# Norm sums, residual order, head of the input projection and softmax division of a two-layer hybrid trunk

## The chip, the cores and the metric

The kernel runs on one core of one Trainium2 chip. The metric is the device time of one execution in microseconds (us), lower is better.

## The reference

All arithmetic is float32. x is (1, 512, 1024); there are two layers, and mem is (1, 256, 1024).

```python
for l in range(DEPTH):
    h = rms_norm(x, norm_mix_pre[l])
    (c_q, c_kv, k_rope, ml_q, ml_k, ml_v, ml_o, ml_i, ml_f,
     sw_q, sw_k, sw_v) = jnp.split(h @ w_in[l], splits, axis=-1)
    # A: 8 heads of latent attention, dense causal; B: 4 mLSTM heads, chunkwise;
    # C: 4 heads of dilated window attention; outputs concatenated
    ... # x += rms_norm(concat @ w_out, norm_mix_post)
    ... # x += rms_norm(cross_attention(rms_norm(x, norm_x_pre), rms_norm(mem)), norm_x_post)
    ... # x += rms_norm(swiglu(rms_norm(x, norm_ffn_pre)), norm_ffn_post)

def rms_norm(x, g):
    return x * lax.rsqrt(jnp.mean(x * x, axis=-1, keepdims=True) + EPS) * g
```

The attention of groups A and C ends in `softmax(s) @ v`; the softmax divides by the sum of the exponentials of a query's row.

## The kernel before, in words

**Layout.** Activations are feature-major: x is 8 tiles (index k) of 128 features by 512 tokens. A weight unit is 128 by 1024 floats, the weights of one output tile of 128 features (index m) with its 8 k steps; there are 128 units per layer (N_UNITS). They pass through a ring of RING = 4 slots: SP loads `raw`, ACT copies it rounded to `w_hi`, DVE makes `w_lo = raw - w_hi` (line 1180, `lo_until(n)`), and TensorE does three matmuls per k step, hi by hi, lo by hi, hi by lo (lines 499 to 501, `three`, `project_step`). A slot is free when TensorE has used its unit (`unit_used`); SP loads unit u when the split of unit u - 4 is done. Activations are split alike: ACT makes `h_hi` (`scaled_hi`, line 861), DVE makes `h_lo` (`scaled_lo`, line 1167). A float32 matmul that isn't split shows as two matmul records.

**Norms.** The sum over features of a norm is taken on TensorE. ACT squares the 8 tiles into two buffers of `sq` in turn (`square`, line 869), DVE adds each to `acc` (`add_square`, lines 1159 and 1161), and `norm_sum` (line 546) multiplies ones by `acc` into bank 7; every partition then has the sum. ACT takes Ln and Exp(-0.5 .) of it (`make_rstd`, lines 885 and 887). There are six such norms per layer: mix_pre, mix_post, x_pre, x_post, ffn_pre and ffn_post. For mix_pre and ffn_pre the rstd is applied behind the matmuls, so that these can start before the norm is known. q and kv have sums of their own (`latent_sum`, line 554).

**Gaps.** A sublayer ends in `post` on ACT (square, and copy with gain, of each output tile), then `norm_sum`, `make_rstd`, and `residual` on DVE: y[k] *= rstd (line 1240), x[k] += y[k] (line 1244), with `between(k)` in each turn, here the h_lo of the next sublayer (`ffn_input`, `next_input`) one tile late, and its squares' adds. The next sublayer's first matmuls run k by k over a few units at once: HEAD = 3 units of the input projection, 4 units of the FFN (`gate_up_step`). Their order is written out in the program of each engine, with semaphores between engines. In layer 0 the first units and the x tiles arrive in turn from DMA, and ACT and DVE take two tiles of x behind each unit.

**Behind the head.** The input projection has 10 tiles (IN_FM) in 6 banks. DVE takes each tile (`take`, line 1231) times mix_rstd and does the gates, convolutions and so on between takes; take m first makes the splits up to unit m + 3.

**Paired heads** (groups A and C, 6 pairs per layer, 4 blocks of 128 queries per pair). In step s TensorE makes the scores of two units (`pair_scores`, line 721), DVE masks them and takes the maximum (`pair_mask`, line 1489), ACT takes the exponential with its sum into `stat[:, 1]` (`pair_exp`, line 1066), DVE takes the reciprocal and scales the probabilities (`pair_divide`, lines 1499 and 1500), TensorE transposes them two steps later (`pair_transposes`, line 734), ACT copies them (`pair_copy`, line 1056). After four blocks `pair_out` (line 745) multiplies by v for both heads, each in its own 64 rows of a bank; ACT and DVE split the result into h_hi and h_lo (`pair_hi`, line 1045; `pair_lo`, line 1477). The out projection waits for the last of them.

## Time and profile before

| | |
|---|---|
| median of 3 runs | 1746.42 us (1743.43 to 1747.57) |
| profiled execution | 1746.7 us, span 1744.9 us |
| TensorE busy (matmul) | 1631.1 us, 93% |
| VectorE busy | 981.3 us, 56% |
| ScalarE busy | 737.3 us, 42% |
| mean granted clock of TensorE | 0.971 |
| chain that ended last | TensorE 85%, VectorE 9%, issue 3%, ScalarE 2% |

The span is the time from the first to the last instruction. The chain is followed back from the last instruction, at each step to what released it. The granted clock is 1.00 at 2.4 GHz and 0.50 at 1.2 GHz. PE is TensorE, DVE is VectorE, ACT is ScalarE, SP issues the DMAs. L12 is line 12 of the kernel.

### The profile page before, as it was taken

Reading aid. Unit: us, or ns where it says so; the run is one execution under the profiler, and the core shown is the slowest. Engines: PE = TensorE matmul, PEld = TensorE weight load, DVE = VectorE, ACT = ScalarE, POOL = GpSimd, SP = SyncE. Lnnn points to the kernel's source line nnn. Section 1 sums busy time; section 2 is a strip of 40 time slices with the busy share of each in tenths; the row PEclk is TensorE's granted clock in tenths of the full one; section 3 lists DMA queues with packets and bytes.
Section 4 is the critical chain, followed back from the end, with each engine's and each line's share of the span. In section 5 each row is a group of like instructions: output and inputs, shape, how many; then the busy total and the mean of one; then the engine's idle time right before and its main releaser. Section 6 shows DMA issues by size and latency. Waiting matters only on the chain.

```text
span 1744.9 us, 18819 instructions
## 1 busy us (share of the span) xinstructions
PE 1631.1 (93%) x7044; PEld 1244.2 (71%) x7044; DVE 981.3 (56%) x1612; ACT 737.3 (42%) x1244; POOL 5.7 (0%) x6
## 2 busy tenths in 40 slices
PE   6999889999989999999989998799999899999996
PEld 5765547877768888888767554487768688888884
DVE  5767874674365555532287678657553755555223
ACT  5522664544444444432244227545353444444221
POOL 0000000000000000000000000000000000000000
PEclk9998999999999999999999989999999999999998
DMA  5311003351213333333213110034403123333321
GB/s 223 109 60 37 13 1 109 109 162 55 61 49 97 97 97 107 99 109 97 85 49 109 49 37 1 17 128 146 121 25 88 51 91 101 105 97 101 105 73 48
DMA packets 38826, 144.62 MB, mean 83 GB/s; under 512 B 4304, under 2 KB 4432, under 8 KB 38224
## 3 DMA queue, kind: packets, MB, share of 16 engines
q1 hardware_dynamic: 38736, 143.43, 26.8%
q8 instruction: 56, 0.92, 0.2%
q14 instruction: 34, 0.28, 0.1%
HBM read 141.31 MB, written 2.10 MB: 82 GB/s over the span
## 4 chain that ended last, share of the span: by engine, by line
PE 85%; DVE 9%; issue 3%; ACT 2%; DMA 0%; SPq 0%; DVEq 0%; ACTq 0%
PE bank L499 24%; PE bank L501 24%; PE bank L500 24%; PE bank L721 2%; PE bank L745 2%; PE bank L794 2%; PE bank L784 1%; PE bank L647 1%; PE bank L655 1%; DVE x L1244 1%; PE bank L734 1%; DVE p_mix L1500 1%; DVE tn_x L1209 1%; DVE w_lo L1180 1%; PE bank L546 1%
## 5 line engine op out<-in xcount | busy, mean ns | idle before, releaser
L499 PE MATMUL bank<-h_hi,w_hi 128*128 128x512 f32 x1312 | 529.1, 403 | 41.2 <-DVE h_lo L1167 22.0
L1180 DVE TENSOR_TENSOR w_lo<-raw,w_hi 128x1024 fp32r<-128x1024 f32 x256 | 312.9, 1225 | 441.5 <-ACT w_hi L850 429.2
L500 PE MATMUL bank<-h_lo,w_hi 128*128 128x512 f32 x1312 | 517.6, 395 | 0.0
L501 PE MATMUL bank<-h_hi,w_lo 128*128 128x512 f32 x1312 | 517.3, 394 | 0.0
L850 ACT ACTIVATE w_hi<-raw 128x1024 fp32r<-128x1024 f32 x256 | 268.3, 1050 | 203.5 <-PE bank L501 193.7
L499 PEld LDWEIGHTS bank<-h_hi,w_hi 128*128 128x128 f32 x1312 | 249.7, 190 | 110.3 <-issue 34.4
L500 PEld LDWEIGHTS bank<-h_lo,w_hi 128*128 128x128 f32 x1312 | 250.1, 191 | 54.7 <-issue 3.4
L501 PEld LDWEIGHTS bank<-h_hi,w_lo 128*128 128x128 f32 x1312 | 250.4, 191 | 53.3
L501 PE MATMUL bank<-a_hi,w_lo 128*128 128x512 f32 x352 | 139.1, 395 | 0.0
L499 PE MATMUL bank<-a_hi,w_hi 128*128 128x512 f32 x352 | 139.0, 395 | 0.0
L500 PE MATMUL bank<-a_lo,w_hi 128*128 128x512 f32 x352 | 139.0, 395 | 0.0
L1161 DVE TENSOR_TENSOR acc<-acc,sq 128x512 f32<-128x512 f32 x84 | 58.1, 691 | 103.9 <-ACT sq L869 102.9
L869 ACT ACTIVATE sq<-bank 128x512 f32<-128x512 f32 x48 | 28.7, 598 | 153.9 <-PE bank L501 153.9
L1136 ACT ACTIVATE a_hi<-sq 128x512 fp32r<-128x512 f32 x44 | 27.8, 632 | 140.8 <-DVE sq L1576 140.8
L500 PEld LDWEIGHTS bank<-a_lo,w_hi 128*128 128x128 f32 x352 | 66.1, 188 | 16.1
L501 PEld LDWEIGHTS bank<-a_hi,w_lo 128*128 128x128 f32 x352 | 66.1, 188 | 16.0
L499 PEld LDWEIGHTS bank<-a_hi,w_hi 128*128 128x128 f32 x352 | 66.1, 188 | 16.0
L1131 ACT ACTIVATE acc<-sq 128x512 f32<-128x512 f32 x44 | 27.8, 632 | 110.1 <-DVE sq L1569 110.1
L988 ACT ACTIVATE w_ml<-w_ml 128x512 f32<-128x512 f32 (+3 forms) x32 | 15.0, 470 | 113.3 <-DVE w_ml L1410 113.3
L721 PE MATMUL bank<-k_mla,q_mla 128*128 128x128 f32 (+3 forms) x128 | 43.1, 461 | 5.3 <-DVE stat L1489 5.3
L1056 ACT ACTIVATE pt_mix<-bank 128x128 f32<-128x128 f32 (+3 forms) x96 | 39.4, 438 | 19.9 <-PE bank L734 18.3
L499 PE MATMUL bank<-m_hi,w_hi 128*128 128x256 f32 x128 | 37.9, 296 | 5.7 <-DVE w_lo L1180 5.0
(186 smaller groups left out, 1922.7 us busy)
## 6 DMA issues: line engine op xcount, KB each, us to landing
raw<-w_in SPq DMA_DIRECT2D x256, 512.0 KB, 3.6
x<-x_in SPq DMA_DIRECT2D x4, 512.0 KB, 8.3
mem<-mem_in SPq DMA_DIRECT2D x2, 1024.0 KB, 4.9
out<-x SPq DMA_DIRECT2D x4, 512.0 KB, 2.6
consts<-c_in SPq DMA_DIRECT2D x1, 1728.0 KB, 13.1
mem_sq<-mem_in SPq DMA_DIRECT2D x1, 1024.0 KB, 5.7
gains<-g_in SPq DMA_DIRECT2D x1, 80.0 KB, 3.3
```

The source lines that it names most:

```text
L499: pe.matmul(out_ap, l_hi, r_hi, start=start, stop=False)
L500: pe.matmul(out_ap, l_hi, r_lo, start=False, stop=False)
L501: return pe.matmul(out_ap, l_lo, r_hi, start=False, stop=stop)
L721: pe.matmul(score_ring[u % 4][:, 0:n], hd["q"][:, qb * P:n], hd["k"][:, 0:n], start=True, stop=True).then_inc(mix_at["scored"], 1)
L745: mm = pe.matmul(outs[pair % 2][64 * i:64 * i + 64, kb * P:SEQ], mix_head(2 * pair + i)["v"](kb), pt_mix[:, i, kb, kb * P:SEQ], start=(kb ...
L794: mm = pe.matmul(outs[c][:, :], v_x[:, kb, col:col + P], pt_x[:, head % 2, kb, :], start=(kb == 0), stop=(kb == 1))
L850: act.activation(w_hi[:, s, :], raw[:, s, :], ACT.Copy).then_inc(split_hi, 1)
L869: act.activation(sq[:, c % 2, 0:width], src, ACT.Square).then_inc(squared, 1)
L1056: act.activation(pt_mix[:, i, 0:m, qb * P:(qb + 1) * P], turned[i][:, 0:m * P].rearrange("p (b q) -> p b q", q=P), ACT.Copy).then_inc(mix_ ...
L1131: done(act.activation(sig, gate_up, ACT.Exp, scale=-1.0), act_step)
L1161: ins = dve.tensor_tensor(acc[:, :], acc[:, :], sq[:, c % 2, :], ALU.add)
L1180: dve.tensor_tensor(w_lo[:, s, :], raw[:, s, :], w_hi[:, s, :].bitcast(F32), ALU.subtract)\
```

## The change

- **Norm sums.** DVE adds only the first 7 squares. TensorE multiplies ones by `acc` and then, into the same sum, by the eighth square. The squares' waits are counted anew.
- **Residual.** x[0] is updated ahead of y[1]'s scaling; `ffn_input(k)` and `next_input(k)` make h_lo of tile k in turn k (before: of k - 1), the last split of the ring moves behind the first h_lo, and `make_rstd` goes ahead of that unit's w_hi on ACT.
- **Dummy matmuls.** Behind the sums of x_post and (in layer 0) ffn_post TensorE does four float32 matmuls of 128 by 512 whose result nobody reads (`keep_busy`).
- **Head.** HEAD = 4 units; TensorE waits for the first FFN units one by one. In layer 0 the k steps of the head follow the list FIRST_HEAD, and ACT's squares and DVE's adds come behind all tiles.
- **Paired heads.** `pair_divide` is gone. DVE takes the reciprocals of a pair's 8 units at once (`pair_invert`); behind `pair_out` TensorE spreads them over a bank with 8 matmuls of a broadcast column by the identity; ACT copies that to `rstd` (`pair_spread`), DVE multiplies the pair's output by it into `sq` (`pair_scale`), and h_hi and h_lo are made from `sq`.
- Three small tiles change their place in SBUF.

```diff
-HEAD = 3
+HEAD = 4
...
+FIRST_HEAD = ([(k, m) for k in range(2) for m in range(1)] + [(k, 1) for k in range(2)]
+              + [(k, m) for k in (2, 3) for m in range(2)] + [(k, 2) for k in range(4)]
+              + [(k, m) for k in (4, 5) for m in range(3)] + [(k, 3) for k in range(6)]
+              + [(k, m) for k in (6, 7) for m in range(HEAD)])
...
-                        pe.matmul(norm_bank[:, 0:width], const(C_ONES), acc[:, 0:width], start=True, stop=True)\
-                          .then_inc(norm_summed, 1)
+                        pe.matmul(norm_bank[:, :], const(C_ONES), acc[:, :], start=True, stop=False)
+                        pe.wait_ge(squared, count(squared, layer, squares_before(name) + KT))
+                        pe.matmul(norm_bank[:, :], const(C_ONES), sq[:, (layer * N_SQUARES + squares_before(name) + KT - 1) % 2, :],
+                                  start=False, stop=True).then_inc(norm_summed, 1)
...
+                    def keep_busy(n):
+
+                        for _ in range(n):
+                            pe.matmul(outs[0][:, :], const(C_ONES), const(C_ROPE_Q, SEQ), start=True, stop=True)
...
-                            pe.wait_ge(mix_at["probs"], count(mix_at["probs"], layer, u + 1))
+                            pe.wait_ge(mix_at["exped"], count(mix_at["exped"], layer, u + 1))
...
                         mm.then_inc(mix_at["out"], 1)
+                        pe.wait_ge(mix_inverted, count(mix_inverted, layer, pair + 1))
+                        for qb in range(TB):
+                            for i in range(2):
+                                u = 2 * (TB * pair + qb) + i
+                                mm = pe.matmul(outs[(pair + 1) % 2][64 * i:64 * i + 64, qb * P:(qb + 1) * P],
+                                               stat[:, 2, u:u + 1].broadcast_to([P, 64]), const(C_IDENT),
+                                               start=True, stop=True)
+                        mm.then_inc(mix_spread, 1)
...
+                    def pair_spread(pair):
+
+                        act.wait_ge(mix_spread, count(mix_spread, layer, pair + 1))
+                        act.activation(rstd[:, :], outs[(pair + 1) % 2][:, :], ACT.Copy).then_inc(mix_spread_copied, 1)
...
-                    split_until(U_FF + 4)
                     make_rstd("x_post", D_MODEL)
+                    split_until(U_FF + 4)
...
+                        scale(0)
+                        for k in range(KT):
+                            dve.wait_ge(y_scaled, count(y_scaled, layer, first + k + 1))
+                            done(dve.tensor_tensor(x[:, k, :], x[:, k, :], y[:, k, :], ALU.add), x_updated)
+                            if k + 1 < KT:
+                                scale(k + 1)
+                            if between is not None:
+                                between(k)
...
                     done(dve.memset(conv_in[:, :, 0:3], 0.0), pads_set)
+                    lo_until(HEAD + 1)
                     dve.wait_ge(rstd_ready, count(rstd_ready, layer, 1))
...
+                    def pair_scale(pair):
+
+                        dve.wait_ge(mix_at["out"], count(mix_at["out"], layer, pair + 1))
+                        dve.wait_ge(mix_spread_copied, count(mix_spread_copied, layer, pair + 1))
...
+                        done(dve.tensor_tensor(sq[:, pair % 2, :], outs[pair % 2][:, :], rstd[:, :], ALU.mult), mix_scaled)
...
-                    lo_until(U_FF + RING)
+                    lo_until(U_FF + RING - 1)
 
                     def ffn_input(k):
 
+                        scaled_lo(layer, "ffn_pre", k, G_FFN_PRE)
+                        lo_until(U_FF + RING)
                         if k >= 1:
-                            scaled_lo(layer, "ffn_pre", k - 1, G_FFN_PRE)
                             add_square(layer, "ffn_pre", k - 1)
```

## Rows read from the trace of the kernel before

**Rows 1.** Who waited for whom, TensorE: waiter, releaser, us in total, times, longest.

```profile
PE bank L734 <- DVE p_mix L1500: 13.6, 14, 1.7
PE bank L734 <- DVE tn_mix L1500: 6.2, 8, 1.2
```

**Rows 2.** Timeline of the gap before layer 0's FFN: start, us, engine, line, operation, idle before.

```profile
494.03 0.60 ACT L869 ACTIVATE sq<-bank 128x512 f32<-128x512 f32 x1 [3.31 <-PE bank L501]
...
495.41 1.12 PE L546 MATMUL bank<-acc,consts 128*128 128x512 f32 x2 [1.42 <-DVE acc L1161]
...
497.95 1.29 DVE L1240 TENSOR_TENSOR y_x<-y_x,rstd 128x512 f32<-128x512 f32 x2 [0.47 <-ACT rstd L887]
...
499.17 0.69 DVE L1244 TENSOR_TENSOR x<-x,y_x 128x512 f32<-128x512 f32 x1
...
501.22 0.75 DVE L1167 SCALAR_TENSOR_TENSOR h_lo<-x,gains,h_hi 128x512 fp32r<-128x512 f32 x1
...
502.12 0.77 PE L499 MATMUL bank<-h_hi,w_hi 128*128 128x512 f32 x1 [5.58 <-DVE h_lo L1167]
...
503.79 0.75 DVE L1167 SCALAR_TENSOR_TENSOR h_lo<-x,gains,h_hi 128x512 fp32r<-128x512 f32 x1
...
505.30 0.69 DVE L1240 TENSOR_TENSOR y_x<-y_x,rstd 128x512 f32<-128x512 f32 x1
...
505.91 0.69 DVE L1244 TENSOR_TENSOR x<-x,y_x 128x512 f32<-128x512 f32 x1
...
506.63 0.75 DVE L1167 SCALAR_TENSOR_TENSOR h_lo<-x,gains,h_hi 128x512 fp32r<-128x512 f32 x1
```

**Rows 3.** TensorE in one microsecond: stretch, its length, busy, matmuls, granted clock.

```profile
504.00:505.00 1.00, 1.00 (x4) 0.50 0.00 0
```

**Rows 4.** The chain that ended last, in order of time: start, us, what.

```profile
33.75 0.86 PE bank L546 x2
...
71.95 1.72 PE bank L554 x4
...
523.64 0.86 PE bank L546 x2
...
869.12 1.14 PE bank L546 x2
...
897.51 0.86 PE bank L546 x2
...
932.24 1.72 PE bank L554 x4
...
1354.16 1.14 PE bank L546 x2
...
1383.04 0.86 PE bank L546 x2
```

**Rows 5.** Timeline at the start of the kernel, ACT and DVE.

```profile
7.54 0.72 ACT L861 ACTIVATE h_hi<-x,gains 128x512 fp32r<-128x512 f32 x1 [1.98 <-DMA x<-x_in]
...
8.38 0.75 DVE L1167 SCALAR_TENSOR_TENSOR h_lo<-x,gains,h_hi 128x512 fp32r<-128x512 f32 x1 [1.45 <-ACT h_hi L861]
```

**Rows 6.** Timeline behind the head of layer 1, DVE.

```profile
899.85 0.69 DVE L1231 TENSOR_TENSOR q_mla<-bank,mix_rstd 128x512 f32<-128x512 f32 x1 [4.43 <-ACT mix_rstd L887]
...
906.41 1.23 DVE L1180 TENSOR_TENSOR w_lo<-raw,w_hi 128x1024 fp32r<-128x1024 f32 x1
```

**Rows 7.** Timeline at the x_pre norm of layer 0, DVE.

```profile
359.12 1.54 DVE L1209 SCALAR_TENSOR_TENSOR tn_x<-x,gains,rstd 128x512 f32<-128x512 f32 x2 [2.13 <-ACT rstd L887]
```

**Rows 8.** Timeline and groups by form, paired heads, layer 0.

```profile
221.76 2.37 PE L745 MATMUL bank<-pt_mix,v_mla 128*64 128x512 f32 x16
...
272.35 0.50 PE L499 MATMUL bank<-h_hi,w_hi 128*128 128x512 f32 x1 [1.50 <-DVE h_lo L1477]
...
L745 PEld LDWEIGHTS bank<-pt_mix,v_mla 128*64 128x64 f32 x128 | 8.5, 136 | 12.9 <-issue 7.4 <-ACT pt_mix L1056 4.4
```

**Rows 9.** TensorE's share and clock, last 16 us of the stage (same columns, all engines).

```profile
254.80:271.00 16.20, 13.04 (x61) 6.29 (x60) 7.40 (x24) 7.91 (x23) 0.00 (x0) 0.75 0.01 2
```

More of the change, by code:

```diff
@@ L226, with added_before @@
 N_SQUARES = sum(k for n, k in NORMS if n not in LATENT)
+SUMMED = [n for n, _ in NORMS if n not in LATENT]
+N_ADDED = (KT - 1) * len(SUMMED)
+def added_before(name):
+    return (KT - 1) * SUMMED.index(name)
 N_NORMED = sum(k for _, k in NORMED)
@@ L568, in _ @@
                         pe.wait_ge(emptied_act, count(emptied_act, layer, 0))
-                    for k in range(KT):
-                        after_norm("mix_pre")(k)
-                        for m in range(HEAD):
-                            project_step("in", m, k, tiles(h_hi), tiles(h_lo))
+                    for k, m in [(k, m) for k in range(KT) for m in range(HEAD)] if layer else FIRST_HEAD:
+                        if m == 0:
+                            after_norm("mix_pre")(k)
+                        project_step("in", m, k, tiles(h_hi), tiles(h_lo))
                     pe.wait_ge(consts_loaded, 16)
@@ L836, in _ @@
                     norm_sum("ffn_post")
+                    if layer + 1 < DEPTH:
+                        keep_busy(4)
             @block.scalar
@@ L1189, in _ @@
                     scaled_lo(0, "mix_pre", k, G_MIX_PRE)
+                for k in range(KT):
                     add_square(0, "mix_pre", k)
@@ L1237, in residual, with scale @@
                         first = scaled_before(name)
-                        for k in range(KT + 1):
-                            if k < KT:
-                                dve.tensor_tensor(y[:, k, :], y[:, k, :], rstd[:, :], ALU.mult)\
-                                   .then_inc(y_scaled, 1)
-                            if k >= 1:
-                                dve.wait_ge(y_scaled, count(y_scaled, layer, first + k))
-                                done(dve.tensor_tensor(x[:, k - 1, :], x[:, k - 1, :], y[:, k - 1, :], ALU.add),
-                                     x_updated)
-                                if between is not None:
-                                    between(k - 1)
+                        def scale(k):
+                            dve.tensor_tensor(y[:, k, :], y[:, k, :], rstd[:, :], ALU.mult).then_inc(y_scaled, 1)
+                        scale(0)
+                        for k in range(KT):
+                            dve.wait_ge(y_scaled, count(y_scaled, layer, first + k + 1))
[4 more added lines that the diff above has]
+                                between(k)
                     def tiles(t):
@@ L1476, in pair_lo @@
                         dve.wait_ge(mix_at["out_hi"], count(mix_at["out_hi"], layer, pair + 1))
-                        done(dve.tensor_tensor(h_lo[:, tile, :], outs[pair % 2][:, :], h_hi[:, tile, :].bitcast(F32),
+                        done(dve.tensor_tensor(h_lo[:, tile, :], sq[:, pair % 2, :], h_hi[:, tile, :].bitcast(F32),
                                                ALU.subtract), mix_at["out_lo"])
```

85 lines of the change are left out of this document (50 added, 35 removed).

## The prediction

> **What bounds the kernel now.** I read the waits of TensorE first. The two lines of the softmax division are the largest item that the change touches outside the gaps: 13.6 + 6.2 = 19.8 us over both layers, in which transposes wait for a scaled tile [rows 1]. Then the timeline of one gap, from the last x_post square to the first matmul of the FFN. The reader is to see a chain in which every link starts when the one before lands: square 494.03, sum 495.41, scaling 497.95, residual 499.17, h_lo 501.22, matmul 502.12 [rows 2]. From there a new h_lo comes every 506.63 - 503.79 = 2.84 us [rows 2], and the clock that TensorE was granted is the lower of its two levels, 1.2 GHz, with four matmuls in a microsecond; before the fall it had done nothing but the 1.12 us of the norm sum since 494.0 [rows 2, 3]. Last the chain of waits, which gives the milestones: the norm sum behind the head at 33.75 and 897.51, the latent sum behind tile 8 of the input projection at 71.95 and 932.24, the ffn_pre sum at 523.64 and 1383.04 [rows 4]. Outside gaps, heads and attention TensorE sets the pace.
>
> The sum is made against the profiled execution, 1746.7 us (span 1744.9, 1.8 around it); the median of the runs is 1746.42, so I take 0.3 off at the end. A measurement of this kernel tells 0.2%, 3.5 us, from no change.
>
> **Price of a tile.** 932.24 - 897.51 = 34.73 us hold one norm matmul (0.86), eight one-column matmuls (about 1.0, estimated) and six tiles [rows 4], so a tile costs 5.45 and three matmuls, one k step, 0.68.
>
> **Norm sums.** Each of 12 gets a second matmul of 0.86 [rows 4]. In a gap the matmul over acc runs under the square, and the one over the square starts when the square lands, about 0.69 after 494.03, and not 495.41 - 494.03 = 1.38 after it [rows 2]: 0.69 won. Elsewhere TensorE or what waits for the sum pays 0.86.
>
> **The gap before the FFN.** Scale, scale, add took 499.17 - 497.95 = 1.22; scale and dependent add take about 0.72 (the step from an add to its reader, 505.91 to 506.63): 0.50 won. From the add to h_lo it was 501.22 - 499.17 = 2.05. Now ACT starts h_hi 0.72 after the add, and h_lo comes 8.38 - 7.54 = 0.84 later [rows 5]: 1.56, 0.49 won. The first matmul comes at 502.12 - 0.69 - 0.50 - 0.49 = 500.44. The four dummy matmuls (3.4 us) fill 495.6 to 499.0, so I expect 2.4 GHz there. They end 1.4 us ahead of the h_lo that TensorE needs, and cost nothing; if the sum came 1.4 later they would stand in the way. The Trainium skill (page "TensorE: Matmul & The Clock Gate", section "What's actually happening") says that the throttled state is the default and activity releases it; by that rule alone the gap would also give back its slow matmuls, 1.6 us here. The trace agrees on the fall.
> But VectorE becomes the limit. A tile's period was 2.84, of which the scale took 505.91 - 505.30 = 0.61 [rows 2]; now the scale hides inside the 0.84 wait for h_hi: 2.84 - 0.61 + 0.84 = 3.07, against 4 x 0.68 = 2.72 of TensorE. The last w_lo split, until now hidden before the rstd, goes behind the first h_lo (1.23 by itself [rows 6]; I take 1.14 to the next start, an estimate, since neighbours overlap by some 0.1 where the reader is another engine). SP asks for a unit's weights when the split of four units before is made, so these loads start about 3 us later; they are used some 20 us on, and their cover is large. First h_lo 499.54, split from 500.32, second add 501.46, second h_lo 503.02, eighth 503.02 + 6 x 3.07 = 521.44. Its first three matmuls end 0.90 + 0.68 later, 523.02, where it was 523.64: 0.62 won. In layer 1 the gap sits 1354.16 - 495.41 = 858.75 later [rows 2, 4], so 1381.77 against 1383.04: 1.27 won. Less 2 x 0.86 for ffn_pre: **+0.2**.
>
> **The gap before layer 1.** It begins 869.12 - 495.41 = 373.71 after the other [rows 2, 4]. Eighth h_lo 895.15, its matmuls from 896.05, four units each, sum at N = 898.77, where three units got there at 897.51. Behind it: 1.72 for two matmuls, tile 4, the one-column matmuls, then tile 5, whose split VectorE makes only after its third take. That was 906.41 - 899.85 = 6.56 after the first take, and the take 899.85 - 897.51 = 2.34 after the sum [rows 4, 6]; now N + 3.20 + 6.56 - 1.14 (tile 4's split is made ahead) = N + 8.62, usable 1.33 later (a split and 0.1), where TensorE comes at N + 8.15. A stall of **1.8** that no head of three had. Latent sum at N + 1.72 + 5 x 5.45 + 1.0 + 1.8 = N + 31.8 = 930.5, against 932.24: **+1.7**.
>
> **The first head.** TensorE starts at 8.38 + 0.85 = 9.23 as before [rows 5], 0.85 being the 0.75 of h_lo and 0.1. With the squares moved behind all splits, ACT and VectorE make h_lo and w_lo faster than TensorE uses them in the new order. 32 steps take 21.8; the first 4.4 us at half clock add 2.2 (an estimate by the 3 us from 502.12 past 504 that it stayed low with dense work [rows 2, 3]; bounds 1.7 and 3.9), waiting for the second split 0 to 0.5. N = 33.5, latent sum at N + 31.8 + 3.5 (the memory's eight matmuls: 71.95 - 33.75 less 34.73) = 68.8, against 71.95: **+3.2** (1.5 to 3.9).
>
> **Sums in the dense part, and the waits added.** mix_post and x_pre stand in series: the second rstd is followed at once by VectorE, which had waited 2.13 for it at 359.12 [rows 7], and its h_lo chain ends last. 2 x 2 x 0.86 = **-3.4**; a gain in its place is excluded, the last add dropped was ahead of time. The new waits of ACT's squares on the previous sum stand behind an rstd that needed the same sum, so nothing queues there. The end of the kernel wins 0.69 and loses 7 x 0.12 (0.72 for 0.61, a dependent pair): **-0.15**.
>
> **The paired heads.** The division moves behind the product. VectorE loses 48 reciprocals and 48 scalings per layer, and of the 9.9 us of waits per layer [rows 1] I give back 6.8, an estimate: two waits of up to 0.7 in each pair, a pair more of them in the first and the last; the rest returns as waits for ACT, which must wait for the spread and copy it before the next pair's copies and exponentials, queued behind. VectorE's new wait for the last exponential of a pair has only the mask of scores behind it that TensorE has not made yet: nothing. Against it 8 matmuls of 64 by 128 per pair, which no row shows. Lower bound: the product's eight have 2560 columns in 2.37 us [rows 8], at its rate 1024 columns take 0.92. Upper bound: 16 loads one after the other, 16 x 0.136 = 2.2 [rows 8]. Their columns are short as the loads are, so I take 1.3, six times 7.8. At the end of the stage the out projection waited 1.50 [rows 8]; a copy of 512 columns on ACT (0.6 to 0.7, like ACT's other passes) and a scaling on DVE (0.72) more make 2.9: 1.4 lost. 6.8 - 7.8 - 1.4 = -2.4 per layer. The stage already ran at 0.75 of the clock in its last 16 us [rows 9]; a longer wait at its end may cost more, denser work before it may save: -0.3 each (bounds -3 and +3). Both layers: **-5.4**.
> The Trainium skill (same page, section "Part 3: Packing small matmuls — row/col tiling") says that matmuls in different column groups run at once, but that a weight load overlaps a matmul only when its row group differs. The first half agrees with the product, 2.37 us for columns that one by one would take five norm matmuls' time, 4.3. The second, which speaks against this change since all rows are used, would make the price the upper bound or more; in the product loads do hide.
>
> **Sum.** 0.2 + 1.7 + 3.2 - 3.4 - 0.15 - 5.4 = -3.9: 1746.7 + 3.9 - 0.3 = **1750.3 us**.
>
> **Rivals.** (1) Faster than before: the spread is cheap. At 0.92 each 12 x 0.38 = 4.6 us come back, and if the denser stage keeps its clock, 16.2 x 0.25 = 4.0 less what the tail still loses, say 3 per layer: 1750.3 - 4.6 - 6 = 1739.7. It decides on this side once the spread and the clock together give back 7.4. For: the product's rate. Against: short matmuls, the end's longer wait. 0.24.
> (2) Loads in series, 2.2 each: 12 x 0.9 more, 1761. For: nothing in the product shows 128 columns alone. Against: loads there hide. 0.12.
> (3) The reorder does not slow VectorE (period 2.84): 6 x 0.23 = 1.4 us more in each of three gaps, 1746. For: the parts sum to it. Against: the 0.84 must pass between two instructions of one tile. 0.10.
> **How the numbers follow.** My forecast has 0.54. Its own range is 1746 to 1755 (the bounds of the first head, the stall ahead of tile 5, and the clock in the pairs), half of it within 0.2% of 1746.4. Over all I give 1740 to 1758, which leaves out (2) and the far part of (1). Faster: (1), 0.24. Within 0.2%: 0.27 of the forecast and (3), 0.37. Slower: 0.27 and (2), 0.39.
>
> **What would show it.** First FFN matmul 6.4 us after the last square's start (was 8.1), at full clock, h_lo period 3.07; N near 33.5 and 898.8; a wait of 1.8 for w_lo ahead of tile 5; x_pre rstd 1.7 later against the end of the out projection; the spread's duration; transposes that no longer wait for VectorE. Wrong if the spread is under 1 us or over 2, or if the stall ahead of tile 5 is absent.

## The result and the profile after

The changed kernel takes 1736.17 us (median of 6 runs, 1733.40 to 1738.99) against 1746.58 of the kernel before (6 runs); the ratio is 0.9945, 95% interval 0.9932 to 0.9957. Measured again beside later kernels it was 1737.34 us, 0.9947 (0.9929 to 0.9966). It is faster by 0.5%, some 9.5 us; the forecast was 1750.3, and the measured time lies below the whole range. The profiled run took 1733.7 us (span 1731.9), 13.0 less than the profiled run before, so part of what two profiles differ by is chance. A second profile of the changed kernel took 1740.4 us: its two stages of paired heads took 76.27 us each, where they take 73.37 in the profile shown here.

The chain that ended last, changed kernel (start, us, what), against [rows 4]:

```profile
33.48 0.86 PE bank L563 x2
42.05 1.24 DVE w_lo L1233
...
70.48 1.72 PE bank L573 x4
...
518.91 0.89 PE bank L563 x2
...
891.56 0.87 PE bank L565 x2
899.26 1.24 DVE w_lo L1233
924.20 1.72 PE bank L573 x4
```

The sum behind the first head came at 33.48 (forecast 33.5), the latent sum at 70.48, only 1.5 earlier than before. The chain now passes through a split on VectorE in both layers, at 42.05 and 899.26: the stall ahead of tile 5 that the forecast had at 1.8 us.

The gap before the FFN of layer 0 (timeline: start, us, engine, line, operation, idle before), against [rows 2]:

```profile
490.54 0.60 ACT L909 ACTIVATE sq<-bank 128x512 f32<-128x512 f32 x1 [3.33 <-PE bank L518]
491.20 1.12 PE L565 MATMUL bank<-sq,consts 128*128 128x512 f32 x2
492.15 3.60 PE L580 MATMUL bank<-consts 128*128 128x512 f32 x8
...
493.73 0.69 DVE L1294 TENSOR_TENSOR y_x<-y_x,rstd 128x512 f32<-128x512 f32 x1 [5.19 <-ACT rstd L927]
494.46 0.69 DVE L1299 TENSOR_TENSOR x<-x,y_x 128x512 f32<-128x512 f32 x1
...
495.19 0.72 ACT L897 ACTIVATE h_hi<-x,gains 128x512 fp32r<-128x512 f32 x1 [0.54 <-DVE x L1299]
...
495.95 0.75 DVE L1220 SCALAR_TENSOR_TENSOR h_lo<-x,gains,h_hi 128x512 fp32r<-128x512 f32 x1
496.73 1.22 DVE L1233 TENSOR_TENSOR w_lo<-raw,w_hi 128x1024 fp32r<-128x1024 f32 x1
496.80 0.47 PE L516 MATMUL bank<-h_hi,w_hi 128*128 128x512 f32 x1 [1.05 <-issue]
...
499.36 0.75 DVE L1220 SCALAR_TENSOR_TENSOR h_lo<-x,gains,h_hi 128x512 fp32r<-128x512 f32 x1
...
502.09 0.75 DVE L1220 SCALAR_TENSOR_TENSOR h_lo<-x,gains,h_hi 128x512 fp32r<-128x512 f32 x1
```

From the last square to the FFN's first matmul it is 496.80 - 490.54 = 6.26 us, where it was 8.09 (forecast 6.4). The sum starts 0.66 behind the square, the add follows its scaling by 0.73, and the dummies of L580 run from 492.15 to 495.75. VectorE's h_lo comes 2.73 behind the one before (499.36 to 502.09) and 3.00 later on (forecast 3.07). The split of the last unit, at 496.73, stands behind the first h_lo, as forecast. In the microsecond that had the lower clock [rows 3], the clock is up (stretch, its length, busy, matmuls, granted clock, DMA):

```profile
504.00:505.00 1.00, 1.00 (x6) 1.00 0.00 0
```

The paired heads. First the waits of TensorE (us in total, times, longest), against [rows 1]; then the end of the stage in layer 0, against [rows 8]; then the clock of the stage's end and of the 3.5 us behind it, against [rows 9] (stretch, its length, busy time of PE, PEld, which is the weight loads, DVE, ACT and POOL, then clock, DMA):

```profile
PE bank L758 <- ACT pt_mix L1105: 10.6, 18, 1.2
```

```profile
260.00 2.37 PE L769 MATMUL bank<-pt_mix,sw_v 128*64 128x512 f32 x16 [0.74 <-ACT pt_mix L1105]
262.21 1.04 PE L777 MATMUL bank<-consts,stat 128*64 128x128 f32 x16
263.30 0.60 ACT L1095 ACTIVATE rstd<-bank 128x512 f32<-128x512 f32 x1 [3.35 <-PE bank L777]
264.09 0.69 DVE L1542 TENSOR_TENSOR sq<-bank,rstd 128x512 f32<-128x512 f32 x1 [6.12 <-ACT rstd L1095]
...
266.30 0.79 PE L516 MATMUL bank<-h_hi,w_hi 128*128 128x512 f32 x1 [3.05 <-DVE h_lo L1548]
```

```profile
254.80:266.30 11.50, 5.42 (x50) 3.46 (x48) 3.49 (x8) 6.80 (x16) 0.00 (x0) 1.00 0.00 0
266.30:269.80 3.50, 3.50 (x8) 2.79 (x9) 0.00 (x0) 0.10 (x1) 0.00 (x0) 0.51 0.70 222
```

The two lines of [rows 1] are gone, 19.8 us; in their place stand 10.6 us for ACT's copies. The spread (L777, 16 records for 8 matmuls) takes 0.97 us to the next instruction inside the stage (220.47 to 221.44 in layer 0), and 1.04 as a row. The chain at the end is the forecast's: spread, copy, scale, h_hi, h_lo, a wait of 3.05 where it was 1.50. The last product runs at full clock, 2.37 us; the out projection behind the wait starts at half clock, its matmuls 0.43 us apart.

These rows alone do not say why the kernel became faster and not slower. The largest difference between the traces lies in a stretch that the forecast did not touch. From the ffn_pre sum to the ffn_post sum it was 345.64 and 345.71 us in the two layers (523.48 to 869.12 in layer 0, the records of the sum over acc) and is 341.32 and 341.31 now, about 0.8 of which is only the new norm sums (the sum over acc starts earlier, and ffn_pre has a matmul more). The groups by form (count | busy us, mean ns of one), before and after:

```profile
L500 PE MATMUL bank<-h_lo,w_hi 128*128 128x512 f32 x1312 | 517.6, 395 | 0.0
L499 PE MATMUL bank<-a_hi,w_hi 128*128 128x512 f32 x352 | 139.0, 395 | 0.0
```

```profile
L517 PE MATMUL bank<-h_lo,w_hi 128*128 128x512 f32 x1312 | 517.1, 394 | 0.0
L516 PE MATMUL bank<-a_hi,w_hi 128*128 128x512 f32 x352 | 136.9, 389 | 0.0
```

The matmuls over h_lo are as they were; those over a_hi (the down projection) went from 395 to 389 ns. Their starts say the same, before and after:

```profile
760.21 0.40 PE L501 MATMUL bank<-a_hi,w_lo 128*128 128x512 f32 x1
760.44 0.39 PE L499 MATMUL bank<-a_hi,w_hi 128*128 128x512 f32 x1
760.67 0.40 PE L500 MATMUL bank<-a_lo,w_hi 128*128 128x512 f32 x1
```

```profile
760.10 0.39 PE L516 MATMUL bank<-a_hi,w_hi 128*128 128x512 f32 x1
760.33 0.39 PE L517 MATMUL bank<-a_lo,w_hi 128*128 128x512 f32 x1
760.55 0.39 PE L518 MATMUL bank<-a_hi,w_lo 128*128 128x512 f32 x1
```

Averaged over the records of a stretch, the distance from start to start in the down projection was 233.3 ns and is 226.7 ns, at full clock in both; in gate and up it is 226.7 in both. 1056 matmuls by 6.6 ns are 7.0 us.

### The profile page after: what moved, and what is told of

It reads as the page before. It is cut to its first block, busy times and chain, and to the rows that moved or that the text cites. A ratio compares the mean times of both kernels' runs of the same rounds, so it can differ in the third digit from the quotient of the medians.

```text
span 1731.9 us, 19052 instructions
## 1 busy us (share of the span) xinstructions
PE 1643.7 (95%) x7284; PEld 1258.7 (73%) x7284; DVE 933.6 (54%) x1432; ACT 739.2 (43%) x1256; POOL 5.7 (0%) x6
## 4 chain that ended last, share of the span: by engine, by line
PE 81%; DVE 9%; ACT 7%; issue 2%; DMA 0%; SPq 0%; DVEq 0%; ACTq 0%
PE bank L516 23%; PE bank L518 23%; PE bank L517 23%; PE bank L826 2%; PE bank L769 2%; DVE x L1299 2%; PE bank L816 1%; ACT pt_mix L1105 1%; ACT p_mix L1115 1%; PE bank L671 1%; DVE h_lo L1220 1%; PE bank L679 1%; ACT h_hi L897 1%; PE bank L745 1%; DVE w_lo L1233 1%
## 5 line engine op out<-in xcount | busy, mean ns | idle before, releaser
L1214 DVE TENSOR_TENSOR acc<-acc,sq 128x512 f32<-128x512 f32 x72 | 49.7, 691 | 75.9 <-ACT sq L909 75.0
L897 ACT ACTIVATE h_hi<-x,gains 128x512 fp32r<-128x512 f32 x32 | 22.8, 723 | 41.6 <-DVE x L1299 38.8
```

Source lines behind the costliest of these rows:

```text
L897: act.activation(h_hi[:, k, :], x[:, k, :], ACT.Copy, scale=gains[:, layer, g + k:g + k + 1])\
L1214: ins = dve.tensor_tensor(acc[:, :], acc[:, :], sq[:, c % 2, :], ALU.add)
```

## The experiments

All ratios are against the kernel before, run beside. "From start to start" is the mean over the records of one stretch of a trace.

**The move alone.** The three small tiles that change their place in SBUF, and nothing else:

```
         gains = sb("gains", [P, DEPTH, N_GAINS])
+        mem_rstd = sb("mem_rstd", [P, N_MEM])
+        stat = sb("stat", [P, 3, MIX_UNITS])
+        acol = sb("acol", [P, TB, ML_HEADS])
         raw = sb("raw", [P, RING, UNIT])
...
         rstd = sb("rstd", [P, SEQ])
-        mem_rstd = sb("mem_rstd", [P, N_MEM])
-        stat = sb("stat", [P, 3, MIX_UNITS])
-        acol = sb("acol", [P, TB, ML_HEADS])
```

> The kernel before with nothing but three small tiles (mem_rstd, stat, acol: 1024 + 576 + 64 = 1664 B of each partition) allocated ahead of raw instead of behind rstd. Theory A (placement): in the profile of the changed kernel the down-projection's matmuls start every 0.2268 us, in that of before every 0.2335; the move puts w_hi 73,728 B ahead of a_hi instead of 75,392, a whole multiple of 256 instead of 128 more. 1056 such matmuls x 0.0067 = 7.1 us: I expect 1739.5 us and a mean of 389 ns for the matmuls over a_hi and a_lo. Theory B (the pitch comes from something else in the change, the clock or what ACT and VectorE do meanwhile): no change, 1746.6 us, mean 395 ns.

Measured: 1738.41 us, ratio 0.9954 (0.9941 to 0.9967), 7 to 8 us faster. The group of its profile:

```profile
L499 PE MATMUL bank<-a_hi,w_hi 128*128 128x512 f32 x352 | 136.9, 389 | 0.0
```

The stretch from ffn_pre to ffn_post is 342.14 and 342.22 us, 3.5 less in each layer. Theory A holds: the larger part of the whole gain is this move.

**The changed kernel without the move** (the same lines undone):

> The changed kernel with those three tiles back behind rstd, all else kept. Theory A (placement): the 7.1 us are given back, 1743.3 us, mean 395 ns over a_hi and a_lo; the changed kernel would then be worth only 3.3 us without its placement. Theory B: 1736.2 us and 389 ns.

Measured: 1742.53 us, 0.9978 (0.9969 to 0.9987), 395 ns over a_hi and a_lo. As theory A had it. So the rest of the change wins some 3 to 4 us, where my sum had it lose 3.9.

**The division alone.** The kernel before with the paired heads' part of the diff (the new functions pair_invert, pair_scale, pair_spread, the spread's matmuls, pair_divide gone):

```
-                            pe.wait_ge(mix_at["probs"], count(mix_at["probs"], layer, u + 1))
+                            pe.wait_ge(mix_at["exped"], count(mix_at["exped"], layer, u + 1))
...
+                        for qb in range(TB):
+                            for i in range(2):
...
+                                mm = pe.matmul(outs[(pair + 1) % 2][64 * i:64 * i + 64, qb * P:(qb + 1) * P],
+                                               stat[:, 2, u:u + 1].broadcast_to([P, 64]), const(C_IDENT),
+                                               start=True, stop=True)
```

> The kernel before with nothing but the paired heads' softmax division moved behind the product (invert once per pair, spread, scale). Theory A (from the two traces: the stage took 73.6 us before and 69.0 after in layer 0, less 0.9 for the half-speed start of the out projection behind it): 3.7 to 4.6 us faster per layer, 1737 to 1739.5 us, a spread of 0.90 us per pair. Theory B (my forecast on record, spread 1.3 and 5.4 lost in both layers): 1752 us.

Measured: 1746.12 us, 1.0001 (0.9989 to 1.0013). Neither theory: nothing won and nothing lost.

**Tiles between the weights and h_hi.** A direct test of what in the placement counts:

```
         w_lo = sb("w_lo", [P, RING, UNIT], F32R)
+        stat = sb("stat", [P, 3, MIX_UNITS])
+        acol = sb("acol", [P, TB, ML_HEADS])
...
         mem_rstd = sb("mem_rstd", [P, N_MEM])
-        stat = sb("stat", [P, 3, MIX_UNITS])
-        acol = sb("acol", [P, TB, ML_HEADS])
```

> The kernel before with stat and acol (640 B) allocated between w_lo and h_hi instead of behind rstd: w_hi and w_lo stay where they are, h_hi, h_lo, sq, acc and rstd move up by 640 B (128 more than a multiple of 256), mem_rstd and a_hi stay. Theory A1 (what counts is where the moving tile lies relative to the weights, modulo 256 B): the matmuls over h_hi and h_lo go from 0.2268 to 0.2335 us apart, 3936 x 0.0067 = 26 us slower, 1773 us, and those over a_hi stay at 0.2335. Theory A2 (the address of the weights alone, or of a_hi alone, counts): no change, 1746.6 us. Theory B: no change.

Measured: 1768.18 us, 1.0126 (1.0110 to 1.0142), 22 us slower. Its matmuls over h, which were 226.7 ns apart, and their group:

```profile
560.38 0.39 PE L501 MATMUL bank<-h_hi,w_lo 128*128 128x512 f32 x1
560.61 0.40 PE L499 MATMUL bank<-h_hi,w_hi 128*128 128x512 f32 x1
560.84 0.39 PE L500 MATMUL bank<-h_lo,w_hi 128*128 128x512 f32 x1
...
L500 PE MATMUL bank<-h_lo,w_hi 128*128 128x512 f32 x1312 | 524.7, 400 | 0.0
```

233.3 ns from start to start; those over a stayed at 233.3. Later in this trace both are 232.4 (over h from 1420 to 1460 us, over a in layer 1), with every tile where it was. Theory A1: the distance between the tile that streams and the tile that is loaded as weights. Absolute addresses are ruled out by the move alone, where w_hi and h_hi went up together by 1664 B and the matmuls over h kept 226.7.

**Move and division together** (the edits of the first and third experiment):

> The kernel before with the three tiles moved and the division moved, nothing else. With the move alone the kernel took 1738.4 us. The profile of the division alone shows the stage from the first scores to the first matmul of the out projection at 73.4 us in both layers, against 77.2 before (3.8 won in each), the out projection behind it 1.5 longer in each (it starts at half clock behind a wait of 3.0), and the stretch ahead of the stage 2.5 longer in each, with a lower granted clock. Theory C (those 2.5 are what the division does to the kernel, by the clock): nothing won again, 1738.4 us. Theory D (they were that arrangement's luck with the clock): 2 x (3.8 - 1.5) = 4.6 won, 1733.8 us.

Measured: 1736.91 us, 0.9946 (0.9930 to 0.9962). Between the theories: the median is 1.5 us better than with the move alone, which the intervals don't tell from nothing.

**The changed kernel with the old division** (the diff's paired part undone):

> The changed kernel with the division back where it was, all else kept, the move of the tiles too. Theory C (the division wins nothing): 1736.2 us. Theory D: 4.6 slower, 1740.8 us. My forecast on record (it costs 5.4): 1730.8 us.

Measured: 1738.95 us, 0.9955 (0.9936 to 0.9973), 1.6 to 2.8 us slower than with the new one. My recorded price is refuted, and the full 4.6 of theory D is not shown either.

**Without the dummies:**

```
                     norm_sum("x_post")
-                    keep_busy(4)
...
                     norm_sum("ffn_post")
-                    if layer + 1 < DEPTH:
-                        keep_busy(4)
```

> The changed kernel without its four dummy matmuls in the three gaps. Theory E (they hold the clock): the first matmuls of the FFN and of layer 1 run at half speed again as in the kernel before, where the windows of 10 us behind the gaps stood at 0.73, 0.53 and about 0.7 of the clock; 1.6 us by my forecast's figure for each of three gaps, 1741 us. Theory F (the h_lo period of VectorE covers it, or the clock stays up anyway): 1736.2 us.

Measured: 1731.73 us, 0.9920 (0.9903 to 0.9936): not slower, but 4 us faster. The clock fell as theory E says (TensorE by stretches of 2 us behind the gap; length, busy, matmuls, clock, DMA):

```profile
498.00:500.00 2.00, 2.00 (x6) 0.50 0.58 225
500.00:502.00 2.00, 2.00 (x10) 0.91 0.03 8
```

and the gap, from the sum over acc to the ffn_pre sum, grew by 0.2 us only, 28.41 to 28.62. The first k step over four units took 5.1 us at half clock (495.43 to 500.54) and ended 1.8 us behind the moment at which the second h_lo was made. From there TensorE took 2.7 us for a k step and VectorE 3.00 for an h_lo, so TensorE caught up, all but 0.2 us. Theory F for the gap. Where the other 3 to 4 us come from is taken up below.

**Single sums outside the gaps, and an earlier split:**

```
+IN_GAP = ("x_post", "ffn_post")
...
+                        if name not in IN_GAP:
+                            pe.matmul(norm_bank[:, :], const(C_ONES), acc[:, :], start=True, stop=True)\
+                              .then_inc(norm_summed, 1)
+                            return
...
-                            lo_until(m + RING)
+                            lo_until(HEAD + 2 if m == 1 else m + RING)
```

> The changed kernel with two things made otherwise: the norm sums of mix_pre, mix_post, x_pre and ffn_pre are one matmul over the sum of all eight squares again (x_post and ffn_post keep two), and VectorE splits unit 5 ahead of its second take behind the head. By the stages of the two traces each of the eight second matmuls costs TensorE 0.77 to 0.86 us, 6.5 in all; the stall ahead of tile 5 is 1.6 in layer 0, with half speed behind it for about 4 us (1.5 to 2 more), and 1.2 to 1.5 in layer 1: 4.5. I expect 1736.2 - 11 = 1725 us. Rival: the stall goes to tile 6, whose split waits for the convolution (loses the 4.5 again): 1730 us.

Measured: 1727.99 us, 0.9893 (0.9874 to 0.9912), 8 to 9 us faster than the changed kernel where 11 were expected. The stretch from the mix_post sum to the x_pre sum is 0.85 and 0.86 shorter in the two layers, the next one 0.89 and 0.86: the price of a second matmul. From the sum behind the head to the latent sum it went from 37.00 to 33.78 us and from 33.50 to 29.95, of which 0.86 is the sum; so the stall cost 2.4 and 2.7 us, not 1.8. Its idle part is 1.6 to 1.7; the rest is the half clock behind it, in the changed kernel (same columns):

```profile
42.00:43.00 1.00, 0.00 (x0) 1.00 0.00 0
44.00:46.00 2.00, 2.00 (x8) 0.61 0.71 236
46.00:48.00 2.00, 2.00 (x6) 0.54 0.07 27
```

**Dummies at the end of the pairs instead of in the gaps,** on the last kernel:

```
+                    keep_busy(3)
                     pe.wait_ge(mix_at["out_lo"], count(mix_at["out_lo"], layer, MIX_PAIRS))
...
-                    keep_busy(4)
...
-                    if layer + 1 < DEPTH:
-                        keep_busy(4)
```

> The last kernel (single norm sums outside the gaps, unit 5 split early; 1728.0 us) with the four dummy matmuls of the gaps left out and three put behind the last pair's spread, where TensorE waits 3.05 us for h_lo and then runs its first eight matmuls at half speed, 0.43 us apart instead of 0.23, from 266.3 to 269.6. Theory G (these dummies keep the clock, and TensorE is what sets the pace behind them): 1.6 won in each layer, and 0.2 lost in each gap, 1728.0 - 3.2 + 0.6 = 1725.4 us. Rival: as in the gaps, what is won is covered by another engine: 1728 us.

Measured: 1723.60 us, 0.9870 (0.9850 to 0.9889), the fastest median here, 23 us below the kernel before. These dummies write into another bank (`wide[0]`). The out projection starts at full clock (timeline, layer 0):

```profile
258.90 1.04 PE L789 MATMUL bank<-consts,stat 128*64 128x128 f32 x16
259.88 2.84 PE L592 MATMUL bank<-consts 128*128 128x512 f32 x6
263.00 0.50 PE L524 MATMUL bank<-h_hi,w_hi 128*128 128x512 f32 x1 [0.28 <-DVE h_lo L1558]
```

From the start of the last matmul of the products to the mix_post sum it is 51.38 us in layer 0 and 52.11 in layer 1, against 52.07 to 53.37 in the profiles of the same stage without these dummies. The gain is a little above what theory G expected, but two things changed at once, the dummies taken out of the gaps and those put at the end of the pairs. The run with all dummies, further down, keeps the gap dummies and takes 0.9877 against the 0.9893 of the kernel that this one started from: 2.8 us for the dummies at the end of the pairs alone, if two sessions may be compared.

**The changed kernel again:**

> The changed kernel once more, unedited, beside kernels of the later sessions. Without its dummies the kernel took 0.9920 of the time before and with them 0.9945 in another session, while the two profiles differ by 1.5 us and the gaps themselves by 0.2. If the dummies cost nothing and win nothing: 0.9925 to 0.994 here, 1734 us. If they really cost 4 us: 0.9945, 1736.5 us.

Measured: 1737.34 us, 0.9947. It repeats the first measurement, so that taking the gap dummies out won 4 to 5 us in that kernel by the medians; the intervals just touch (0.9903 to 0.9936 without, 0.9929 to 0.9966 with). This profile took 1740.4 us and the one without dummies 1732.1. Of the 8.3 us between them 5.8 lie in the paired heads, hundreds of us behind any gap: 76.27 us in both layers against 73.37.

**64 bytes between,** and **1024 bytes ahead:**

```
         w_lo = sb("w_lo", [P, RING, UNIT], F32R)
+        acol = sb("acol", [P, TB, ML_HEADS])
...
-        acol = sb("acol", [P, TB, ML_HEADS])
```

> The kernel before with acol alone (64 B) between w_lo and h_hi: h_hi and h_lo lie 64 B more than a multiple of 256 from w_hi, w_hi and a_hi stay. Theory A1a (only a whole multiple of 256 gives the short pitch): the matmuls over h_hi and h_lo go to 0.2335 us apart, 1768 us as with 128 B. Theory A1b (128 B is special): they stay at 0.2268, 1746 us. Or a pitch between the two, and a time between.

Measured: 1752.63 us, 1.0036 (1.0019 to 1.0053); 228.9 ns over h, 232.4 over a. A price between.

```
         gains = sb("gains", [P, DEPTH, N_GAINS])
+        mem_rstd = sb("mem_rstd", [P, N_MEM])
         raw = sb("raw", [P, RING, UNIT])
...
-        mem_rstd = sb("mem_rstd", [P, N_MEM])
```

> The kernel before with mem_rstd alone (1024 B) moved ahead of raw: a_hi then lies 74,368 B from w_hi, still 128 more than a multiple of 256. Theory A1 (the remainder modulo 256 counts): no change, 1746 us, mean 395 ns over a_hi and a_lo. Rival (any such move helps, or the tiles moved out of the way of sq and acc do): 1738.5 us, 389 ns.

Measured: 1744.14 us, 0.9995 (0.9982 to 1.0008); 233.3 ns over a, as before. The rival is out: it isn't the moving of tiles that helps, it is the remainder.

**The division undone in the fastest kernel** (paired part of the diff undone, one dummy at the end):

> The fastest kernel so far (1723.6 us: division behind the product, single sums outside the gaps, unit 5 split early, three dummies behind the last spread) with the division put back ahead of the transposes, and one dummy at the end of the pairs for its wait of 1.5. Theory C' (the division saves its structural part once the clock behind it is held): the stretch from the first product to the last is 4.9 shorter with it and the first product comes 1.3 earlier, less a last spread of 0.9 and a wait 1.5 longer: 3.8 per layer, so this kernel takes 1731.2 us. Theory C (it is given back by the clock elsewhere, the stage of the gated heads above all): 1723.6 to 1726 us.

Measured: 1729.63 us, 0.9913 (0.9889 to 0.9938): 6 to 7.5 us slower. The size is near what theory C' gave it, the mechanism isn't shown. The dummies stand behind the last product and hold the clock of the out projection, not of the stage: with the old division the stage took 77.20 and 74.64 us in the two layers, with the new one 73.40 and 76.30, so each had one layer in which the clock fell. From the first product to the last it is 4.9 us shorter with the new division in layer 0, as C' said, and 0.4 in layer 1 (59.45 and 57.09 against 54.56 and 56.72). The two profiles differ by 3.1 us.

**32 and 192 bytes between:**

```
-        eps = sb("eps", [P, 1])
...
         w_lo = sb("w_lo", [P, RING, UNIT], F32R)
+        eps = sb("eps", [P, 1])
```

> The kernel before with eps (4 B, 32 with its padding) allocated between w_lo and h_hi instead of ahead of raw: h_hi lies 32 B more than a multiple of 256 from w_hi, a_hi 160 B more. Theory H (the price rises with the distance from the nearest multiple of 256): about 228 ns from matmul to matmul over h_hi, and 232 over a_hi; 1749 us. Theory I (there are two or three steps): 226.7 or 229.0 over h_hi, 1746 or 1755 us.

Measured: 1778.30 us, 1.0186 (1.0152 to 1.0220); 233.3 ns over h, 234.3 over a. Both theories miss: from matmul to matmul 32 B cost as much as 128. That the kernel takes 10 us more than with 128 B has another part: in its profile the out projection starts at half clock in both layers and takes 51.2 us, against 48.3 in the one with 128 B. It ran twice only.

```
-        eps = sb("eps", [P, 1])
-        one = sb("one", [P, 1])
...
         w_lo = sb("w_lo", [P, RING, UNIT], F32R)
+        stat = sb("stat", [P, 3, MIX_UNITS])
+        acol = sb("acol", [P, TB, ML_HEADS])
+        eps = sb("eps", [P, 1])
+        one = sb("one", [P, 1])
...
-        stat = sb("stat", [P, 3, MIX_UNITS])
-        acol = sb("acol", [P, TB, ML_HEADS])
```

> The kernel before with stat, acol, eps and one (704 B with padding) between w_lo and h_hi: h_hi lies 192 B more than a multiple of 256 from w_hi, and a_hi too. Theory H (distance from the nearest multiple): 229.0 ns over h_hi and over a_hi, 1746.6 + 9 - 4.5 = 1751 us. Theory J (the price rises all the way to 256): 235 ns or more over both, 1780 us.

Measured: 1770.92 us, 1.0144 (1.0109 to 1.0179); 233.3 ns over both. Theory H is out (192 is not 64), and J too. What stands: a whole multiple of 256 B gave the short distance each time, every remainder tried a longer one, 64 the least.

**All dummies:** the gap dummies put back into the fastest kernel, the three at the end of the pairs kept.

> The fastest kernel (1723.6 us, ratio 0.9870, three dummies behind the last spread of each layer) with the four dummies in each of the three gaps back. Theory K (they win what the gaps show, 0.2 each by the changed kernel's profiles, and 0.6 by those of the two fastest): 1722.5 us. Theory L (they cost some 4 us in the stages behind, by the clock, as 0.9920 against 0.9946 says): 1727.5 us. Within 2 us of 1723.6: they do nothing that these runs can tell.

Measured: 1728.04 us (1719.51 to 1728.54), 0.9877 (0.9854 to 0.9900) against 0.9870 (0.9850 to 0.9889). Unclear: the medians say theory L, the intervals cover each other, and the fastest single run of all, 1719.51, is one of these.

**The division alone, with the end held:** the third experiment, and

```
+                    for _ in range(3):
+                        pe.matmul(wide[0][:, :], const(C_ONES), const(C_ROPE_Q, SEQ), start=True, stop=True)
                     pe.wait_ge(mix_at["out_lo"], count(mix_at["out_lo"], layer, MIX_PAIRS))
```

> The kernel before with the division moved and three dummies behind the last spread, old placement, nothing else. Theory M (the half-speed start of the out projection ate a part of the division's gain, 1.4 us in each layer, the rest was the clock's scatter): the stretch from the first scores to the mix_post sum at 120.6 in each layer against 122.1 with the division alone and 124.4 to 125.1 before; 1746 - 8 = 1738 us. Theory C (nothing is won in this kernel, held or not): 1746 us.

Measured: 1742.82 us, 0.9977 (0.9963 to 0.9990), 3.3 to 4 us better than without the dummies. The stretch from the first scores to the mix_post sum is 120.56 in layer 0 and 120.55 in layer 1, as theory M has it; the time is half of what M expected. The trace shows where most of the other half went: from the sum behind the head to the first scores it took 163.4 us in layer 0 and 157.4 in layer 1, in the kernel before 160.8 and 156.5. The program of layer 0 is the same in both up to there; what differs is the clock, 0.857 against 0.889 from the second latent sum to the first scores.

## Why the prediction was wrong, step by step

**The whole, in three factors.** Leaving single parts out gives three comparisons for the move and for the division, and three for all the rest (gaps, head, sums):

| part | comparisons (ratio with / ratio without) | mean |
|---|---|---|
| move of three tiles | 0.9954/1; 0.9946/1.0001; 0.9945/0.9978 | 0.9955, 7.8 us won |
| division | 1.0001/1; 0.9946/0.9954; 0.9945/0.9955 | 0.9994, 1 us won |
| the rest | 0.9978/1.0001; 0.9955/0.9954; 0.9945/0.9946 | 0.9992, 1.3 us won |

Each single ratio is uncertain by 0.1 to 0.2%. My terms for the rest, 0.2 + 1.7 + 3.2 - 3.4 - 0.15, add up to 1.55 us won. That agrees with the 1.3 of the table, which has an uncertainty of 2, but by luck: term by term (below) the traces show 1.4 + 0.6 + 1.5 - 3.2 - 0.2 = 0.1 won, with errors of both signs. Two steps failed.

**The step that failed first: the move wasn't costed at all.** It stood in the section on the change as three tiles changing their place, and the prediction has no term for it and no rival. It is 6 to 8 of the 10 us (8 by the move alone, 6 by leaving it out, and 7.0 by the matmuls' distance in the traces). In the kernel before, a_hi lies 75,392 B behind w_hi, 128 more than a multiple of 256; the move makes it 73,728, a whole multiple. h_hi lies 32,768 B behind w_hi in both. The profile had it: before the change the two groups of the same shape have the same mean, 395 ns, though all the half-speed stretches lie in the first; at full clock the second was slower, and I didn't ask why.

**The step that failed next: the paired heads, -5.4.** By its own terms, for layer 1: TensorE over the stage (length, busy, matmul records, clock), before and after:

```profile
1053.81:1131.01 77.20, 61.49 (x313) 0.93 0.00 1
```

```profile
1046.79:1120.16 73.37, 61.19 (x410) 0.97 0.00 1
```

- *Waits recovered, 6.8.* Idle time went from 15.7 to 12.2 us although the end waits 1.55 longer: 5.1 recovered. The waits for ACT, 5.3 in each layer, are larger than I allowed.
- *The spread, 1.3 each.* 0.97: 5.8 instead of 7.8. It is the lower bound, which I had worked out wrongly: 2.37 us for 2560 columns make 0.95 for 1024, not 0.92.
- *The end, 1.4.* 1.55, right, and then 0.65 to 0.95 more for the half clock of the out projection, 1.5 in the kernel with the division alone.
- *The clock, -0.3 (bounds -3 and +3).* Here the term fell. Busy time went from 61.5 to 61.2 with 5.8 us of spread added: the same other work took 6.1 less. Not all of that is the clock. In the kernel with 1024 bytes ahead the stage of layer 0 has the old division and kept the clock (first row; the second row is its transposes alone, the third those of the changed kernel, same columns):

```profile
192.73:267.28 74.55, 58.86 (x313) 0.98 0.00 1
```

```profile
192.73:267.28 74.55, 20.97 (x120) 0.98 0.00 1
```

```profile
192.92:266.29 73.37, 18.00 (x120) 0.98 0.00 1
```

So the clock is 61.5 - 58.9 = 2.6 of the 6.1. The other 3.5 come at the same clock, and 3.0 of them are the transposes, which are busy for 18.0 us instead of 21.0 now that they wait less often. My sum had counted the waits, but no time of the matmuls around them.

So the stage went from 77.2 to 73.4 us: 2.6 by the clock, and at equal clock 5.1 + 3.5 - 5.8 - 1.55 = 1.2, where my terms had -2.4. Rival (1), a cheap spread and a clock that stays up, was the right mechanism for it, with the wrong companion: the out projection pays a part back. The clock's share differs from run to run. Over all 19 profiles here, with two layers each, the stage with the old division took 74.5 to 74.6 us in 3 of 18 cases and 77.0 to 78.2 in the others; with the new one 73.4 in 14 of 20 and 76.2 to 76.3 in the others. At equal clock the division wins about 1 us a layer; what differs more is how often the clock falls in the last part of the stage, which costs 2.9 (the mean over the last 16 us is then 0.75 to 0.80 instead of 1.00). That the division changes these odds is likely by the counts, but argued and not tested by an experiment of its own. Means of 76.9 and 74.2 less 0.7 to 1.5 behind the stage make 2.4 to 4 us in both layers; the ratios show 1, with an uncertainty of 2. Where dummies hold the clock at the start of the out projection the gain is 4 and 6 us. In the profile with the division alone the stretch ahead of the pairs took 109.8 us in both layers against 107.5 to 108.5 before (second latent sum to first product), at a lower clock. The traces speak for the run and against the kernel: the same stretch with the division took 105.6 and 109.7 us with the tiles moved, and 109.8 and 107.3 with the dummies behind the last spread, and up to its first scores the program of layer 0 has nothing of the division in it.

**The smaller terms.**
- *Gap before the FFN, +0.2.* From the square to the ffn_pre sum over acc 28.37 us in both layers, where it was 29.61 and 30.25; less two sums that is 1.4 won. First h_lo 5.41 behind the square (5.51 forecast), the period 2.96 on average, not 3.07, because h_lo starts 0.76 behind h_hi (0.84 taken from [rows 5], where the engine had been idle). Rival (3) had the period at 2.84; it lies between.
- *Gap before layer 1, +1.7.* 63.93 from square to latent sum against 64.50: 0.6 won. The sum over acc behind the head was 0.6 earlier than forecast, the stall 0.9 dearer (2.7 against 1.8: its wait was 1.66 and right, but the clock falls behind it), and the tiles between the two sums took 0.8 more than my price (29.95 in the kernel without the stall, for which it gives 29.1).
- *First head, +3.2.* The sum at 33.48 was on the forecast, with some luck, for the sum over acc, 33.32 here, is at 33.05 in the second profile and at 32.55 without the dummies; the latent sum came 1.7 late, 1.4 of it by the same two errors: the stall, which I had charged by its idle time, and the tiles' price (the terms I gave, 34.73 less 0.86 and 1.0 over six tiles, make 5.48 and not 5.45, which is 0.15 of it). In the changed kernel without the move the clock stayed up behind the same stall, and that stretch took 35.37 instead of 37.00 us.
- *Sums in the dense part, -3.4.* 0.75 to 0.89 for each of four: right.
- *End of the kernel, -0.15.* 17.8 us from the square to the end of the span before, 18.0 now: right.
- *The dummies cost nothing.* They do hold the clock in the gap, as forecast, but the "1.6 us here" that I set beside the Trainium skill's rule on the throttled state (page "TensorE: Matmul & The Clock Gate", section "What's actually happening") is 0.2: TensorE loses 1.8 us on VectorE in its first k step at half clock and wins nearly all of it back, since VectorE is the slower of the two from then on. That the kernel as a whole was 4 us faster without them is measured, its cause is open; the larger part of the difference between the slower profile with them and the one without lies in the clock of the paired heads.
- *The load rule.* The same page's section "Part 3: Packing small matmuls — row/col tiling" says that a load overlaps only when its row group differs. The spread has all rows in every load, and eight matmuls of 64 by 128 take 0.97 us: no run here shows such a serialisation.

The Trainium skill also says (same page, section "Step-by-step: what each phase is for") that loading the next weights doesn't take SBUF bandwidth from the running matmul. The runs don't agree without a condition: 226.7 or 233.3 ns, by the distance of the two tiles alone, and 233 also from 798 to 800 us in the kernel before, where ACT and VectorE are idle, as elsewhere.

## What to carry to other kernels

When a change moves allocations, cost the move: compare the start-to-start distance of matmuls of one shape over different tiles in the profile before, and if one is longer at the same clock, look at where its tiles lie to each other before anything else. A term for the clock deserves the range that its stage shows over several profiles, and a wait costs its length plus the half-speed work behind it, unless TensorE can catch up on a slower engine. Here dummy matmuls paid where TensorE itself set the pace after the gap (the out projection) and not where it followed another engine (the FFN's start). One profile of each kernel is not enough for effects of a few us: the pair shown first has the clock down in both paired stages before and up in both after, which alone is over 5 us of their 13.

## What the runs showed of the hardware

Distance from the weights' tile (w_hi; w_lo lies 16,384 B on) to the streaming tile, modulo 256 B, and the distance from start to start of 128x128 by 128x512 matmuls at full clock:

| remainder | over h | over a |
|---|---|---|
| 0 | 226.7 ns | 226.7 ns |
| 32 | 233.3 | |
| 64 | 228.9 | |
| 128 | 233.3, in parts of the same trace 232.4 | 233.3, in parts 232.4; 232.4 throughout in the kernel with 64 B between |
| 160 | | 234.3 |
| 192 | 233.3 | 233.3 |

Not expected, and not explained: why 64 costs a third of the others, why with it the three matmuls of a step differ (231.7, 226.0 and 229.0 ns from the one before to h_lo by w_hi, h_hi by w_lo and h_hi by w_hi), and why a remainder of 128 gives 233.3 in one part of a trace and 232.4 in another. That last difference needs no move of a tile: the kernel with stat and acol between shows both over h, 233.3 from 560 to 600 us and 232.4 from 1420 to 1460. 2.9% of each matmul hangs on the remainder, 22 us of this kernel if the tiles over h are laid wrongly. What in the memory or the engine makes the difference no run shows. The clock's scatter is the other finding: the stretches ahead of and in the paired heads differ by 3 to 4 us from one profile to the next of nearly the same kernel (105.6 to 109.8 ahead, 73.4 to 76.3 in them, all with the new division), which is more than the effects of most edits here.
